# A two-block transformer on one core: the sums of squares behind the last down products move to GpSimd

## The reference, cut to what matters

```python
# first block, l = 0 and l = 1
y = (silu(x @ w_gate) * (x @ w_up)) @ w_down
x = layer_norm(ALPHA * x + y, ln_ffn_g[l], ln_ffn_b[l])     # mean and variance over 1024
# second block, behind its last layer
h = h + (relu(hn @ w_up) ** 2) @ w_down
out = h * rsqrt(mean(h * h) + EPS) * ln_final                # mean square over 1024
```

## Time and profile before

| | |
|---|---|
| median of 3 runs | 2390.98 us (2389.67 to 2391.91) |
| profiled execution, its own time | 2389.86 us |
| its span, first to last instruction | 2388.1 us |
| TensorE, matmul busy | 2354.7 us (99%) |
| VectorE busy | 1669.6 us (70%) |
| ScalarE busy | 999.6 us (42%) |
| GpSimd busy | 22.7 us (1%), 39 instructions |
| chain that ended last | TensorE 86%, VectorE 7%, ScalarE 5% |
| mean granted TensorE clock | 0.999 |

### The profile page before, as it was taken

How to read it: one execution, slowest core, us unless ns; L and a number is a source line. 1 busy time by engine, 2 the same in 40 slices (tenths; PEclk the granted TensorE clock), 3 DMA queues, 4 the chain that set the end, 5 groups by cost and what they waited for, 6 DMA issues and landing times.

```text
span 2388.1 us, 30288 instructions
## 1 busy us (share of the span) xinstructions
PE 2354.7 (99%) x12574; PEld 1987.1 (83%) x12574; DVE 1669.6 (70%) x2234; ACT 999.6 (42%) x1414; POOL 22.7 (1%) x39
## 2 busy tenths in 40 slices
PE   8999999999999999999999999999999999999998
PEld 7887888999998887999997786888888777888886
DVE  5998746988778746888888526566656886566566
ACT  4446544644444744544445435322222565222222
POOL 0000000000000000000000000000000000000000
PEclk9999999999999999999999999999999999999999
DMA  5323313232223211322332220233333212222321
GB/s 186 105 91 105 114 45 106 89 106 104 93 105 117 98 43 71 106 92 104 106 106 94 90 105 23 103 119 109 109 126 117 75 54 71 101 94 89 106 96 63
DMA packets 38872, 228.96 MB, mean 96 GB/s; under 512 B 8837, under 2 KB 8917, under 8 KB 12496
## 3 DMA queue, kind: packets, MB, share of 16 engines
q1 hardware_dynamic: 31680, 219.17, 26.3%
q0 software_dynamic: 7056, 7.86, 1.4%
HBM read 221.71 MB, written 5.24 MB: 95 GB/s over the span
## 4 chain that ended last, share of the span: by engine, by line
PE 86%; DVE 7%; ACT 5%; issue 1%; DMA 1%; SPq 0%; DVEq 0%; ACTq 0%
PE bank L779 85%; DVE w_lo L2221 2%; ACT w_hi L1583 1%; DMA w_raw<-weights_in 1%; ACT xs L1676 1%; ACT xh L1614 1%; DVE xl L2244 1%; DVE cacc L2550 1%; PE bank L1516 1%; DVE xs L2359 0%; DVE xs L2339 0%; ACT pr L1953 0%; DVE sum_q L2258 0%; DVE sum_x L2251 0%; DVE xs L2315 0%
## 5 line engine op out<-in xcount | busy, mean ns | idle before, releaser
L779 PE MATMUL bank<-xh,w_hi 128*128 128x512 f32 (+1 forms) x1248 | 440.5, 353 | 13.4 <-DVE w_lo L2772 7.0
L779 PE MATMUL bank<-xl,w_hi 128*128 128x512 f32 (+1 forms) x1248 | 435.8, 349 | 0.0
L779 PE MATMUL bank<-xh,w_lo 128*128 128x512 f32 (+1 forms) x1248 | 435.7, 349 | 0.0
L2221 DVE TENSOR_TENSOR w_lo<-w_raw,w_hi 128x2048 fp32r<-128x2048 f32 x138 | 316.1, 2291 | 166.7 <-ACT w_hi L1583 166.6
L1583 ACT ACTIVATE w_hi<-w_raw 128x2048 fp32r<-128x2048 f32 x138 | 263.2, 1907 | 262.7 <-PE bank L779 257.0
L2315 DVE TENSOR_TENSOR xs<-xs,bank 128x512 f32<-128x512 f32 x448 | 292.5, 682 | 65.3 <-PE bank L779 64.8
L779 PEld LDWEIGHTS bank<-xh,w_hi 128*128 128x128 f32 x1248 | 236.6, 190 | 53.0 <-DVE w_lo L2772 7.0
L779 PEld LDWEIGHTS bank<-xh,w_lo 128*128 128x128 f32 x1248 | 236.7, 190 | 30.6
L779 PEld LDWEIGHTS bank<-xl,w_hi 128*128 128x128 f32 x1248 | 236.8, 190 | 30.1 <-issue 0.5
L779 PE MATMUL bank<-yh,w_hi 128*128 128x512 f32 x576 | 227.3, 395 | 0.2 <-DVE w_lo L2221 0.2
L779 PE MATMUL bank<-yl,w_hi 128*128 128x512 f32 x576 | 224.3, 389 | 0.0
(11 more groups left out here) (325 smaller groups left out, 4290.3 us busy)
## 6 DMA issues: line engine op xcount, KB each, us to landing
w_raw<-weights_in SPq DMA_DIRECT2D x204, 1024.0 KB, 4.9
rel_scratch<-vt POOLq DMA_DIRECT2D x8, 384.0 KB, 20.0
bias<-rel_scratch POOLq DMA_DIRECT2D x8, 256.0 KB, 3.2
y_out<-xs SPq DMA_DIRECT2D x8, 256.0 KB, 2.2
xs<-x_in SPq DMA_DIRECT2D x3, 512.0 KB, 8.8
mk<-mem_in POOLq DMA_DIRECT2D x1, 1024.0 KB, 8.7
window<-consts_in POOLq DMA_DIRECT2D x1, 576.0 KB, 4.0
xs<-x_in SPq DMA_DIRECT2D x2, 256.0 KB, 4.6
```

What stands on the lines that cost most here:

```text
L779: return pe.matmul(dst, a, b, start=start, stop=stop, skip_group_check=adds)
L2221: dve.tensor_tensor(w_lo[:, ring(c)], w_raw[:, c % 2, :], w_hi[:, ring(c)].bitcast(F32), ALU.subtract)\
```

## The change

At `ffnn0`, `ffnn1` and `fin` GpSimd adds squares 0 to 6 into `sum_q`, six adds each time. It waits for its own previous add. ScalarE's squares 2 to 7 wait for GpSimd's adds (`tail_sq_used`) in place of VectorE's; the buffer of two squares stays. VectorE adds tiles 0 to 6 into `sum_x` at `ffnn0` and `ffnn1`. TensorE takes `sum_x` and tile 7, then `sum_q` and square 7: 4 products at `ffnn0` and `ffnn1`, 2 at `fin`. Other norms keep their sums.

```diff
+            def sum_of_squares(name):
+                n = TAILS[name]
+                for k in range(1, KT - 1):
+                    pool.wait_ge(sem["tail_sq_ready"], KT * n + k + 1)
+                    if k > 1:
+                        pool.wait_ge(sem["tail_sq_used"], (KT - 2) * n + k - 1)
+                    pool.tensor_tensor(sum_q[:, :], sq[:, 0, :] if k == 1 else sum_q[:, :], sq[:, k % 2, :], ALU.add)\
+                        .then_inc(sem["tail_sq_used"], 1)
...
             const(window[:, :, :, :].rearrange("p a g t -> p (a g t)"), "window", window_loaded)
+            sum_of_squares("ffnn0")
+            sum_of_squares("ffnn1")
             pool.wait_ge(unit_used, ITEM[UNITS["glr"]])
...
+            sum_of_squares("fin")
...
+            def tail_norm_sums(name, keys_, has_mean=True):
+                mean_, sq_ = (name, "mean"), (name, "sq")
+                if has_mean:
+                    wait_free(pe, mean_)
+                    seen.next("sum_x_ready")
+                    mm(bank(mean_)[:, :], ones[:, :], sum_x[:, :], True, False)
+                    wait_drained(pe, keys_[KT - 1])
+                    full(mm(bank(mean_)[:, :], ones[:, :], xs[:, KT - 1, :], False, True), mean_)
+                wait_free(pe, sq_)
+                pe.wait_ge(sem["tail_sq_used"], (KT - 2) * (TAILS[name] + 1))
+                mm(bank(sq_)[:, :], ones[:, :], sum_q[:, :], True, False)
+                pe.wait_ge(sem["tail_sq_ready"], KT * (TAILS[name] + 1))
+                full(mm(bank(sq_)[:, :], ones[:, :], sq[:, (KT - 1) % 2, :], False, True), sq_)
...
-                late_norm_sums(f"ffnn{l}", last_down_keys(f"ffn{l}"))
+                tail_norm_sums(f"ffnn{l}", last_down_keys(f"ffn{l}"))
...
+            def tail_square(name, k, src):
+                if k >= 2:
+                    act.wait_ge(sem["tail_sq_used"], (KT - 2) * TAILS[name] + max(k - 2, 1))
+                give(act.activation(sq[:, k % 2, :], src, ACT.Square), "tail_sq_ready")
...
                 for k in range(KT):
                     add(k, keys[k])
-                    sums_between(k, keys, True)
+                    for j in {2: (1,), 3: (2,), 4: (3,), 5: (4,), 6: (5, 6)}.get(k, ()):
+                        wait_drained(dve, keys[j])
+                        if j < KT - 2:
+                            add_to_sum_x(j, xs_at)
+                        else:
+                            dve.wait_ge(dve_steps, sum_step[0])
+                            give(dve.tensor_tensor(sum_x[:, :], sum_x[:, :], xs[:, j, :], ALU.add), "sum_x_ready")
...
-                    else:
-                        sums_between(k, keys, False)
```

More of the change, by code:

```diff
@@ L445 @@
     "sq_used",
+    "tail_sq_ready", "tail_sq_used", "sum_x_ready",
     "mean_ready",
@@ L668, in col @@
             return prm[:, c:c + 1]
+        TAILS = {"ffnn0": 0, "ffnn1": 1, "fin": 2}
         LN_TAIL = {"mixn0": "mix", "mixn1": "mix", "xan0": "xa", "xan1": "xa", "ffnn0": "ffn", "ffnn1": "ffn"}
@@ L1558, in _ @@
             mlp("mlp1", tile_and_sums("r3"))
-            late_norm_sums("fin", None, False)
+            tail_norm_sums("fin", None, False)
         @block.scalar
@@ L1776, in ffn @@
                     wait_drained(act, last_down_keys(name)[k])
-                    square(k, xs[:, k, :])
+                    tail_square(name.replace("ffn", "ffnn"), k, xs[:, k, :])
                     if name == "ffn1" and k == KT - 2:
@@ L1798, in mlp @@
                     else:
-                        square(k, xs[:, k, :])
+                        tail_square("fin", k, xs[:, k, :])
             def recurrence():
```

## The result

| | before | after |
|---|---|---|
| median, us | 2390.65 (8 runs, 2389.67 to 2391.91) | 2398.89 (8 runs, 2398.07 to 2400.36) |
| ratio, 95% interval | | 1.0035 [1.0026, 1.0044] |
| profiled execution, its own time | 2389.86 | 2400.36 |
| span | 2388.1 | 2398.6 |
| mean granted clock | 0.999 | 0.996 |

The changed kernel is 8.2 us slower, and the interval lies wholly above 0.2%. That is inside the range (2386.6 to 2401.0) and well outside the forecast's own (2390.5 to 2395.6): it said +3.05 us and "no change" as the likeliest. The profiled execution of after stands 10.5 us above the one of before, but 2.3 us of that were there ahead of the change's first place (bank 2 of `ffnn0` is added at 752.76, before at 750.45).

The account below looks back on a forecast made before the run. TensorE, busy 99%, was taken to lose time only in waits: for VectorE's bank 7 at `ffnn0` and `ffnn1`, own products ending `fin`. Terms 1.6 + 1.2 + 0.25 = +3.05 us gave 2394.0 us, range 2386.6 to 2401.

Parts of the forecast that it names:

- What bounds the kernel: VectorE's add of bank 7, 2.45 us behind the banks at `ffnn0`, `ffnn1` alike; TensorE's own three products at `fin`.
- VectorE would be 1.8 us earlier with nothing in its way: At `ffnn0` and `ffnn1`, bank 7 would be added 1.8 us earlier if VectorE, with fewer adds, were undisturbed.
- Turns, only for adds of tiles: At `ffnn0` and `ffnn1`, GpSimd's adds and VectorE's adds of tiles alternate in full: bank 7 +1.6 and +1.2 us.
- P = 1.1 and 0.07 for a handover: Assumed time in us of one GpSimd 128x512 add, bounds 0.54 and 1.43, and of each handover, at all three places.
- 2370.0 + 6P: End of GpSimd's chain of adds at `fin`, P being one add's time: 2376.6, TensorE's product 0.24 us later.
- I count no loss of clock: TensorE's 4.3 us wait at `ffnn0` keeps its clock; a loss would cost 3.4 us over four products, partly covered.
- ISA: Rival: GpSimd's first add at `ffnn0` is delayed by the new instruction or first use; 2395.5 us, chance 0.05.
- held banks: Rival: VectorE's adds of banks are held too, at all three places; +6.5 on top, about 2400.5 us, chance 0.06.
- side by side: Rival: GpSimd's and VectorE's adds do not disturb each other; -3.35 us, 2387.6 us, chance 0.29 including nearly so.
- GpSimd becomes the bound: Rival: six longer GpSimd adds in a row, each turn paid, at all three places; +8.8, 2399.8 us, chance 0.24.
- long adds: Rival: GpSimd's adds take up to 1.43 us and its chain bounds all three places; +8.8 us, chance 0.24.
- Slower by over 0.2%: Outcome for the whole kernel: slower by more than 4.8 us, chance 0.36; no change had 0.59, faster 0.05.

Follow-up runs that it names:

- e5_copy_and_memset: The changed kernel, but GpSimd copies squares at `ffnn0` and only fills `sum_q` at `ffnn1`, without their sums of squares; 2388.85 us, ratio 0.9992 to before.
- e4_array_busy: The changed kernel plus 16 unused TensorE products ahead of the product of `sum_x` at `ffnn0` and `ffnn1`; 2395.64 us, ratio 1.0021 to before.

## Why the range held and the forecast was too low

*What bounds the kernel.* Right: the add of bank 7 is what counts at the gated layers as long as the clock holds, TensorE's products at `fin`.

*VectorE would be 1.8 us earlier with nothing in its way.* Right, and shown by `e5_copy_and_memset`: 1.77 at both places for bank 7, 1.77 and 1.70 for the variance.

*Turns, only for adds of tiles.* Right. The forecast's pace of 0.60 + 1.10 = 1.70 us for a tile is the one measured, 1.71. It is so for a reason that I did not have: GpSimd's add takes 1.29, not 1.10, but behind another's operands it needs only 1.11 more, since its start overlaps. That the pace came out is luck. Bank 7 came 1.82 and 1.46 us later, forecast 1.6 and 1.2; the remaining 0.2 to 0.3 I have not split up; the first add of tiles, at 1.68 the longest, meets a whole add of GpSimd.

By the Trainium skill (SBUF — State Buffer, Who interferes with whom) such an instruction of VectorE and one of GpSimd that reads are exclusive, and the second is blocked until the first is done. The traces agree, with 0.56 and 1.11 behind the other's end, and with memsets that hold nobody.

*P = 1.1 and 0.07 for a handover.* One pass of 512 columns is 0.50 us by the two memsets of the earlier trace rows carried on in a line, and not 0.54; it measured 0.53, so this did no harm. P itself was mis-sized, and this is the term of `fin`. An add is 1.29 and a handover 0.13 (6.98 for five, with four handovers). The forecast's own formula, 2370.0 + 6P with 0.15 for TensorE, gives 2377.95 for P = 1.30; four handovers of 0.13 in place of 0.07 make that 2378.19, and after shows 2378.19 on the same footing (2387.18 less 8.99, by which bank 2 of `fin` came later, 2377.88 against 2368.89). So the root lost 1.50 in place of 0.24. The forecast took a middle of bounds without a row for a read, and the bounds were right.

By the Trainium skill (GPSIMD Engine Reference, Performance versus the Vector engine) the estimate was 1.17 us; measured 1.29, so it too was short, by 0.12.

*"I count no loss of clock."* This is the step that failed, and the largest single miss: 3.08 us of the 8.2 at `ffnn1`, the variance's 4.54 less bank 7's 1.46. Another 0.35 came behind the variance of `ffnn0`; `e4_array_busy` kept the clock there and has 0.69 more than before on that stretch, so no run shows that it is the clock's. I had foreseen a wait of 4.3 us, and it was 4.50 and 4.14; I had priced the loss at 3.4. What was wrong was to read the one place of the earlier trace rows, where the clock lasted 5.4 us behind the last product, as a bound. At `ffnn1` it had begun to fall within 4.1 us, and in `e4_array_busy` it fell at `fin` behind a wait of 2.54. Also missed: at `ffnn1` only two rests of 1.14 and 2.28 stand ahead of the variance, so slow products lie open there, while at `ffnn0` `w_hi` and `w_lo` cover most of them. That cover I had mentioned, and not worked out by place.

By the Trainium skill (TensorE: Matmul & The Clock Gate, HAM oscillation — how this bites in real kernels) idle gaps of TensorE bring its clock down, and a kernel is better ordered so that they do not arise. The traces agree at the gated layers: gaps of 4.50 and 4.14 us brought 0.50, and `e4_array_busy`, with most of the gap filled, kept 1.00.

*ISA, held banks, side by side.* All three rivals fell: the first add starts at 753.20, 0.08 behind its squares (they ended at 753.12); adds of banks stay at 0.67 to 0.69; adds of tiles are not undisturbed. GpSimd had been idle for 14.62 us ahead of that add, so whatever `ISA` cost it lies inside.

*GpSimd becomes the bound.* Its time, 2399.8, is the nearest of all to the result, but for another reason. With P = 1.30 in its formula it has +2.8, +2.4 and +1.2, 6.4 in all; the queues gave 1.82 + 1.46 + 1.50 = 4.8, the clock 3.1, and 0.35 stays open. That the measured time lies inside the range is luck too: the range reached so far up for long adds and held banks, and 3.1 us of the loss belong to neither.

*The chances.* "Slower by over 0.2%" had 0.36 and should have had more than half: P near the upper bound or the clock, either alone, leads there from +3.05 (with the clock as measured 3.05 + 3.08 = 6.1), and two independent dangers on one side were each counted as the less likely.

## What to carry to other kernels

Moving an elementwise chain to GpSimd can pay only where VectorE, while it runs, does nothing that reads two operands from the memory; otherwise the two take turns, here 1.71 us for a tile in place of 1.20. Even where nothing disturbs it, as at `fin`, the chain must not become the bound: one add per 1.43 us was slower than one bank per 1.36. Before taking products from TensorE, or making it wait longer, work out how long it stands still and what its next products cost at half the clock, for each place by itself; one place that kept its clock is no bound for another, nor for the same place in the next execution. An operand kept in a bank escapes the turns here (0.68 throughout), which was seen for the adds of banks; sums of tiles kept in a bank were not tried.

## What the runs showed of the hardware

- GpSimd, 128x512 float32: add of two operands 1.29 us, copy 0.60, fill 0.53; a dependent add starts 0.13 behind the end of the one before. A copy costs hardly more than a fill (+0.07), the second operand 0.69; I had taken about 0.44 for each.
- VectorE's instructions with two operands in the memory and GpSimd's that read it take turns, whole instruction by whole instruction in the order of issue. GpSimd's read is needed (a fill held nobody, 0.69 and 0.52) and one stream of it is enough (a copy: 0.55 and 0.48 behind the other's end). Rests of 2048 columns stretched from 2.29 to 2.76, 2.87 and 3.35.
- The granted clock fell at different distances from the last matmul: later than 764, with TensorE idle since 759.52; within 1297 to 1298, with TensorE idle since 1293.91; at about 2384 in before, with TensorE idle since 2378.64. It can fall when TensorE already works again: at `ffnn0` the products ran from 764.02, and at `fin` of `e4_array_busy` from 2383.44, behind a wait of only 2.54 us, while three other executions with that wait kept 1.00. Sixteen small products in the gap (3.73 us of it) kept it at 1.00 at both gated layers.
